# A hybrid decoder step on one core: order of the first loads, pacing of VectorE's convolution, a later norm, and two copies moved to ScalarE

## The chip, the cores and the metric

The kernel runs on one core of a Trainium2 chip. The metric is the device time of one execution in microseconds (us). PE is TensorE (PEld its weight loads), DVE is VectorE, ACT is ScalarE, POOL is GpSimd, and SP is the queue that issues most of the DMAs.

## The reference, cut to what matters

One layer of a decoder trunk over 16 meta tokens and 512 prompt tokens, and 8 sequences of 4 sample tokens (560 tokens in all), width 1024:

```python
proj = rmsnorm(h) @ w_in                 # [q | k | v | z | a | b | glu_in]
qkv = silu(causal_dwconv(qkv, 4 taps))   # then l2norm of q and k per head
# gated delta rule, 4 heads of 128, prompt in chunks:
L = strict(kb @ k.T * decay);  sol = solve(I + L, [v * beta | kb * exp(G)])
v_new = u_v - w_k @ S;  o = (q * exp(G)) @ S + (q @ k.T * decay) @ v_new
S = S * exp(G_last) + (k * exp(G_last - G)).T @ v_new
# the other 512 channels:
c = causal_dwconv(glu, 31 taps) + b;  c = silu(layernorm(c))
h = h + [o, c] @ w_out
h = h + peer(rmsnorm(h))                 # top-k over 128 x 128 experts, dense over all of them
```

## The kernel before, in words

The work is done in stages. (1) **Head**: five tiles of 112 rows of x are loaded, squared and normalised, transposed on PE, and split into a high and a low part in fp32r (ACT writes the high part with `xhigh`, DVE the low part with `xlow`). Weights come in blocks of up to 256 columns; `high(b)` on ACT and `low(b)` on DVE split block b in the same way, and PE makes three products a tile. (2) **Blocks 0 to 7**: the scalars a and b, the first glu block, and six q/k/v blocks, back to back on PE; ACT evacuates each unit (half of the tokens for 128 columns), DVE makes the 4-tap convolutions. After a block, `scalars(b)` makes one part of the gates or of the row norms of q and k. (3) **Mixer**: blocks 8 to 12 (glu 1, glu 3, glu 2, z, z) and the delta rule of five chunks (chunk 0 of 48 rows, chunks 1 to 4 of 128), the sample sequences, the layer norm of the convolution, and the first output units. (4) The output and query projections, the top-k, and (5) a dense pass over the experts with their gathers, about two thirds of the time.

In the mixer every engine runs one fixed order. Each strand of work (a chunk, the sample tokens, the norm, the late blocks) is a generator that yields the name of its next step, and `side_by_side` takes the step with the smallest **turn**, a hand-written number. A chunk's step has the turn `FIRST[ci] + LEVEL[n]`, with FIRST 4.2, 13.5, 30.5, 41.3 and 44.8. Half a unit of a late block takes one turn (`lin` + 0.6), so the five late blocks fill turns 0.6 to 39.6. The norm's steps stand in `NORM_AT`: `ls` (PE sums over channels, 46), `lc` (DVE subtracts the mean), `lv0` to `lv3` (ACT squares a channel tile at the same turn at which PE wants it), `lr`, `lm`, `ln` (49.6). All engines share the turns, and a semaphore per engine counts finished steps.

The 31-tap convolution of four channel tiles is 4 x 31 = 124 **pieces** on DVE, one instruction over 528 columns each (L1892 and L1894). `CONV_BY` gives how many are done after each of the blocks 2 to 7; block 7 brings them to 31. In the mixer, `feed` adds up to two pieces after every DVE step while the turn is under 40 and one after that, as far as the glu blocks so far allow (31 pieces for each). The sample tokens' taps (`conformer_seqs`) follow inside `glu`: one product over 992 columns, a reduction, a bias.

The inverse of a chunk's triangular block is built from powers: `p2`, `p4`, `p8` and their transposes `pt2`, `pt4`, then `n`, `nt`, `n2`, `nt2`, `nt4`. PE makes each in a PSUM bank, and ACT copies the plain ones into SBUF, DVE the transposed ones, `nt4` apart. `free_bank` makes PE wait until the engine named in `chunk_groups` has read a bank's earlier content.

At the end of block 7, the last `scalars` on PE makes the column sums for the row norms of q and k (one-column products, L949); DVE adds eps, ACT takes the square root, DVE inverts (`row_scales`, L1856), all in the first turns of the mixer.

## Time and profile before

| what | value |
|---|---|
| runs | 1883.71 us median of 3 (1883.66 to 1886.05) |
| the profiled execution | 1889.95 us, span of its trace 1888.2 us |
| PE / PEld busy | 95% / 93% of the span |
| DVE busy | 74% |
| ACT / POOL busy | 38% / 36% |
| mean granted TensorE clock | 0.975 |

Busy shares are averages over stages with different limits, so the stages have to be read one at a time: the granted clock and the busy time of each engine in a stretch, and which wait ends last at a step. A granted clock of 1.00 is 2.4 GHz and 0.50 is 1.2 GHz; a value between is a mixture of both within the stretch.

### The profile page before, as it was taken

The page shows a single profiled execution, that of the slowest core. Times are in us where ns is not written, and L with a number is a line of the kernel's source. Part 1 is how long each engine was busy: PE and PEld are TensorE (multiplying, and loading weights), DVE is VectorE, ACT ScalarE, POOL GpSimd, SP SyncE. Part 2 cuts the span into 40 slices and gives each one's busy share as a digit, 9 for nine tenths or more (in the row PEclk, how much of TensorE's full clock was granted, in tenths as well). Part 3 has the DMA queues.
Part 4 walks back from the last instruction along what each step waited for, and adds up shares of the span by engine and source line. Part 5 has one row for each costly group of instructions (what it writes and reads, how often), then busy time and mean ns, then how long its engine had stood idle before and what let it go on. Part 6 is the DMA issues. An engine that isn't in the chain of part 4 may idle for free.

```text
span 1888.2 us, 29407 instructions
## 1 busy us (share of the span) xinstructions
PE 1802.2 (95%) x11505; PEld 1752.5 (93%) x11505; DVE 1393.0 (74%) x2528; ACT 712.0 (38%) x1244; POOL 672.4 (36%) x438
## 2 busy tenths in 40 slices
PE   6997879799899999999999999999999999999998
PEld 5997779789899999999999999999999999999997
DVE  4876896565499999999966657526878788887753
ACT  4535333642333343334344333333333333333332
POOL 3000000000000467868777677771344333333100
PEclk9988899889999999999999999999999999999999
DMA  7211001045132368888998989999999999999831
GB/s 209 68 45 45 32 1 52 1 100 151 41 112 90 126 238 277 266 294 298 321 312 302 314 291 308 316 329 403 322 387 379 348 341 359 357 340 345 318 115 37
DMA packets 190706, 424.33 MB, mean 225 GB/s; under 512 B 11162, under 2 KB 119222, under 8 KB 180320
## 3 DMA queue, kind: packets, MB, share of 16 engines
q1 hardware_dynamic: 153256, 287.47, 44.0%
q0 software_dynamic: 37312, 134.97, 20.4%
q8 instruction: 92, 1.51, 0.3%
q14 instruction: 46, 0.38, 0.1%
HBM read 360.76 MB, written 62.06 MB: 224 GB/s over the span
## 4 chain that ended last, share of the span: by engine, by line
PE 59%; DVE 15%; issue 2%; POOL 1%; ACT 0%; DMA 0%; DVEq 0%; POOLq 0%
PE psum L1292 31%; PE psum L1271 21%; PE psum L1259 3%; PE psum L901 3%; DVE junk L2395 2%; DVE besti L2258 1%; DVE sring L2262 1%; DVE besti L2270 1%; DVE best L2266 1%; DVE best L2254 1%; PE psum L906 1%; DVE oh L2385 1%; DVE WR L1786 1%; DVE eqx L2322 1%; DVE pick L2333 1%
## 5 line engine op out<-in xcount | busy, mean ns | idle before, releaser
L1271 PE MATMUL psum<-xT,WS 128*128 128x416 f32 x3072 | 595.0, 353 | 4.6 <-POOL WS L841 4.6
L1292 PE MATMUL psum<-AR,WS 128*128 128x416 f32 x3072 | 580.5, 350 | 2.6 <-DVE AR L2466 2.6
L1292 PEld LDWEIGHTS psum<-AR,WS 128*128 128x128 f32 x3072 | 574.2, 187 | 8.9 <-DVE AR L2466 3.0
L1271 PEld LDWEIGHTS psum<-xT,WS 128*128 128x128 f32 x3072 | 572.1, 188 | 10.6 <-POOL WS L841 6.2
L841 POOL TENSOR_TENSOR WS<-RAWP,WS 128x1024 fp32r<-128x1024 f32 x128 | 309.7, 2430 | 720.8 <-ACT WS L1686 620.2
L906 PE MATMUL psum<-xT,WR 128*128 128x280 f32 (+1 forms) x1968 | 282.2, 304 | 15.0 <-DVE ss L1795 7.8
L832 POOL DMA_INDIRECT rowg<-in_expert_v,idx x128 | 182.5, 1426 | 315.4 <-DVE acc L2409 307.6
L906 PEld LDWEIGHTS psum<-xT,WR 128*128 128x128 f32 x1968 | 270.4, 200 | 16.7 <-DVE ss L1795 8.1
L1696 ACT ACTIVATE WS<-RAWP 128x1024 fp32r<-128x1024 f32 x128 | 135.6, 1059 | 332.5 <-PE psum L1292 332.5
L2459 DVE TENSOR_TENSOR WS<-RAWP,WS 128x1024 fp32r<-128x1024 f32 x128 | 156.7, 1224 | 114.6 <-ACT WS L1696 114.6
L1723 ACT ACTIVATE actA<-psum 128x416 f32<-128x416 f32 x128 | 66.4, 519 | 404.9 <-PE psum L1271 404.6
L2395 DVE CUSTOM_DVE_ANT_0 junk<-rowg,psum 128x1024 bf16<-128x1024 f32 x128 | 155.9, 1218 | 51.2 <-DMA rowg<-in_expert_u_rows,idx 43.3
L832 POOL DMA_INDIRECT rowg<-in_expert_u_rows,idx x128 | 165.9, 1296 | 41.0 <-issue 22.8
L2409 DVE SCALAR_TENSOR_TENSOR acc<-rowg,coef,acc 128x1024 f32<-128x1024 f32 x128 | 163.9, 1281 | 2.9 <-DMA rowg<-in_expert_v,idx 0.5
L2385 DVE TENSOR_TENSOR oh<-iotab,pairs 128x2048 bf16<-128x2048 bf16 x52 | 96.1, 1847 | 91.8 <-PE psum L1259 90.9
L1686 ACT ACTIVATE WS<-RAWP 128x1024 fp32r<-128x1024 f32 x128 | 134.4, 1052 | 0.0
L1894 DVE SCALAR_TENSOR_TENSOR cT<-gext,dwcols,cT 128x528 f32<-128x528 f32 x120 | 92.3, 769 | 4.2
L2388 DVE TENSOR_TENSOR ohg<-oh,pairs 128x3072 bf16<-128x3072 bf16 x52 | 91.5, 1759 | 1.8
L2457 DVE TENSOR_TENSOR act<-act,Gt 128x416 f32<-128x416 f32 x128 | 74.9, 585 | 13.0 <-DMA act<-act_dram 9.5
L1748 ACT ACTIVATE AR<-act 128x416 fp32r<-128x416 f32 x128 | 69.0, 539 | 39.0 <-DVE act L2457 39.0
L2466 DVE TENSOR_TENSOR AR<-act,AR 128x416 fp32r<-128x416 f32 x128 | 74.9, 585 | 6.6 <-ACT AR L1748 6.5
L1259 PE MATMUL psum<-ohg,oh 128*128 128x128 bf16 x1248 | 78.7, 219 | 0.0
(373 smaller groups left out, 1610.2 us busy)
## 6 DMA issues: line engine op xcount, KB each, us to landing
RAWP<-in_expert_u SPq DMA_DIRECT2D x64, 1024.0 KB, 6.8
RAWP<-in_expert_v SPq DMA_DIRECT2D x64, 1024.0 KB, 7.9
act_dram<-actA SPq DMA_DIRECT2D x128, 208.0 KB, 4.3
gate_dram<-gblk SPq DMA_DIRECT2D x26, 1024.0 KB, 10.4
act<-act_dram SPq DMA_DIRECT2D x64, 416.0 KB, 8.3
Gt<-gate_dram SPq DMA_DIRECT2D x16, 1664.0 KB, 9.7
RAW<-in_w_in SPq DMA_DIRECT2D x8, 1024.0 KB, 5.4
RAW<-in_w_query SPq DMA_DIRECT2D x8, 1024.0 KB, 8.4
```

Of the source, the lines that this page charges most:

```text
L832: pool.indirect_dma_start(out=rowg[:, s_ % 4, :], out_offset=None, in_=table, in_offset=bass.IndirectOffsetOnAxis(ap=idx[:, s_ % PAIRS:s_ ...
L841: pool.tensor_tensor(ws(n)[:, 1], raw(n), ws(n)[:, 0].bitcast(F32), ALU.subtract).then_inc(u_low, 1)
L906: last = mm(bank[u % 4][:, 0:hw], W[:, pw, kt, m * P:(m + 1) * P], xT[:, px, kt, side * hw:(side + 1) * hw], **go)
L1259: last = mm(bank[4 + g % GBANKS][:, k * NK:(k + 1) * NK], oh[:, b % 2, 0, i, :], ohg[:, b % 2, x, i, :], start=(x == 0), stop=(x == 2))
L1271: last = mm(bank[e % 2][:, 0:TD], ws(e)[:, pw, kt * P:(kt + 1) * P], xT[:, px, kt, TSP:TPE], start=(kt == 0 and i == 0), stop=(kt == KT - ...
L1292: last = mm(bank[dt][:, 0:TD], ws(NK + e)[:, pw, dt * P:(dt + 1) * P], AR[:, e % 4, pa, :], start=(e == 0 and i == 0), stop=(e == NK - 1 a ...
L1686: act.activation(ws(n)[:, 0], raw(n), ACT.Copy).then_inc(u_high, 1)
L1696: act.activation(ws(n)[:, 0], raw(n), ACT.Copy).then_inc(v_high, 1)
L2385: chain(tt(by_two(oh[:, i]), keys_, per_token(0, 2), ALU.is_equal))
L2395: dve.tensor_tensor_reduce(junk[:], rowg[:, s_ % 4, :], xnP, 1.0, 0.0, ALU.mult, ALU.add, sdot[:, s_:s_ + 1]).then_inc(dot_done, 1)
L2409: dve.scalar_tensor_tensor(acc[:], rowg[:, s_ % 4, :], coef[:, s_:s_ + 1], acc[:], ALU.mult, ALU.add).then_inc(axpy_done, 1)
L2459: tt(ws(NK + e)[:, 1], raw(NK + e), ws(NK + e)[:, 0].bitcast(F32), ALU.subtract).then_inc(v_low, 1)
```

## The change: what it does

- SP issues all five row tiles of x before the weights of block 0 (before: the weights stood between tiles 2 and 3). POOL issues its two large small-parameter loads (`sconf`, `sqkv`) last, and waits for the last row tile before them. ACT and DVE take the rows of tiles 3 and 4 ahead of the split of block 0.
- The row norms of q and k: PE's last sums come after the second unit of block 7, `row_squares` on DVE between the block's two channels, ACT's roots and the last two SiLUs before `high(9)`, and `row_scales` after `low(9)` and ahead of the mixer.
- DVE's late work in pieces: `low` of blocks 10, 11 and 12 in four parts at turns 1.5 apart; the sample taps of a late glu in two products, a turn apart, and a reduction at a third turn.
- Taps by places: block 7 no longer brings the pieces to 31 (they stay at 26), and `feed` follows `due(turn)`, with at most 3 pieces a step.
- The norm of the convolution starts at turn 48.5 and not at 46, and its squares get turns of their own, ahead of the sums; `onb` and `on` of the first three outputs move back with it.
- The copies of `pt2` and `nt2` go from DVE to ACT.

```diff
-CONV_BY = {2: 5, 3: 10, 4: 16, 5: 21, 6: 26, 7: CC}
+CONV_BY = {2: 5, 3: 10, 4: 16, 5: 21, 6: 26}
...
-                  "onb": {SAMPLE: 47.2, 1: 48.2, 2: 49.2, 3: 56.1, 4: 59.2},
-                  "on": {SAMPLE: 47.9, 1: 48.9, 2: 49.9, 3: 56.6, 4: 60.5}}
-        NORM_AT = {"ls": 46, "lc": 46.05, "lv0": 47.1, "lv1": 47.6, "lv2": 48.1, "lv3": 48.6, "lr": 48.7,
-                   "lm": 49.1, "ln": 49.6}
+                  "onb": {SAMPLE: 48.9, 1: 50.1, 2: 51.1, 3: 56.1, 4: 59.2},
+                  "on": {SAMPLE: 49.6, 1: 50.7, 2: 51.7, 3: 56.6, 4: 60.5}}
+        NORM_AT = {"ls": 48.5, "lc": 48.55, "sq0": 49.3, "sq1": 49.35, "lv0": 50.3, "lv1": 50.8, "sq2": 50.85,
+                   "lv2": 51.3, "sq3": 51.32, "lv3": 51.75, "lr": 51.85, "lm": 52.3, "ln": 52.8}
...
-                 ("pt2", (V, "pt2")), ("t1", (V, "t1")), ("p4", (A, "p4")), ("pt4", (V, "pt4")), ("t2", (V, "t2")),
+                 ("pt2", (A, "pt2")), ("t1", (V, "t1")), ("p4", (A, "p4")), ("pt4", (V, "pt4")), ("t2", (V, "t2")),
...
-                g += [("n", (A, "n")), ("nt", (V, "nt")), ("n2", (A, "n2")), ("nt2", (V, "nt2")),
+                g += [("n", (A, "n")), ("nt", (V, "nt")), ("n2", (A, "n2")), ("nt2", (A, "nt2")),
...
             for t in range(NTB):
                 load_rows(t)
-                if t == 2:
-                    load_weights(0)
+            load_weights(0)
...
+                    (dtb[:, 0:HEADS], dt_bias.to_broadcast([P, HEADS])),
+                    (dtb[:, HEADS:], a_log.to_broadcast([P, HEADS])),
                     (sconf[:], state_conf[0].rearrange("(r b) t c -> (b t) r c", r=2)),
-                    (sqkv[:], state_qkv[0].rearrange("b t c -> (b t) c")),
-                    (dtb[:, 0:HEADS], dt_bias.to_broadcast([P, HEADS])),
-                    (dtb[:, HEADS:], a_log.to_broadcast([P, HEADS]))):
+                    (sqkv[:], state_qkv[0].rearrange("b t c -> (b t) c"))):
+                if n == 8:
+                    pool.wait_ge(x_in[NTB - 1], 16)
                 pool.dma_start(dst, src).then_inc(small_in, 16)
...
-                linear(b)
-                scalars(b)
+                if b == LATE - 1:
+                    linear(b, lambda n: scalars(LATE - 1) if n == 1 else None)
+                else:
+                    linear(b)
+                    scalars(b)
...
             xhigh(1, 1)
-            high(0)
-            xhigh(1, 2)
             square(1, 4)
             root(1, 4)
+            xhigh(1, 2)
+            high(0)
...
-                while done < 2 * sum(x[0] == "qkv" for x in BLOCKS[:b]):
+                if b == LATE - 1:
+                    V.wait(act, "qk2")
+                    fn(tok[:, RQ], tok[:, RQ], ACT.Sqrt)
+                    fn(tok[:, RK], tok[:, RK], ACT.Sqrt, "rqk")
+                while done < 2 * sum(x[0] == "qkv" for x in BLOCKS[:b + (b == LATE - 1)]):
...
+                yield "pt2", ci
+                if ci:
+                    V.wait(act, "Lo", ci)
+                take("pt2", M[3][0:c, :, 0:c])
...
+                yield "nt2", ci
+                take("nt2", M[5][:])
...
+            xnorm(1, 3)
+            xlow(1, 2)
             low(0)
-            xlow(1, 2)
-            xnorm(1, 3)
...
+            def late_lows():
+
+                for b in range(LATE + 1, first["out"] - 1):
+                    n = sum(x[2] for x in BLOCKS[b + 1][2])
+                    for i in range(4):
+                        yield ("lin", 2 * (UNIT0[b] - UNIT0[LATE]) + 1.6 + 1.5 * i), LIN
+                        A.wait(dve, "high", b + 1)
+                        k = slice(2 * i, 2 * i + 2)
+                        op(tt(WR[:, (b + 1) % 2, 1, k, 0:n], RAW[:, SLOT[b + 1], k, 0:n],
+                              WR[:, (b + 1) % 2, 0, k, 0:n].bitcast(F32), ALU.subtract), "low", b + 1)
+
+            def late_glus():
...
+                        yield ("lin", k + 8.5), LIN
+                        glu(b)
+                        yield ("lin", k + 9.9), LIN
+                        for i in range(2):
+                            if i:
+                                yield ("lin", k + 10.9), LIN
+                            seqs_product(c, 4 * i, 4 * i + 4)
+                        yield ("lin", k + 11.9), LIN
+                        seqs_sum(c)
...
-                yield "pt2", ci
-                op(dve.tensor_copy(sq_(M[3]), src("pt2")), "pt2", ci)
...
-                    if n == "r1":
-                        yield "nt2", ci
-                        op(dve.tensor_copy(sq_(M[5]), src("nt2")), "nt2", ci)
...
+            def due(at_):
+
+                return 26 + int(min(max(at_ - 5, 0), 5) + 2 * min(max(at_ - 9.6, 0), 18.4)
+                                + 2.6 * min(max(at_ - 28, 0), 12) + 3.2 * max(at_ - 40, 0))
+
             def feed(at_):

-                conv_to(min(pieces[0] + (2 if at_ < LINEAR_END else 1), CC * gated[0]))
+                conv_to(min(max(pieces[0], due(at_)), pieces[0] + 3, CC * gated[0]))
```

## Rows read from the trace of the kernel before

**Rows 1.** Windows: stretch, length, busy PE PEld DVE ACT POOL, PEclk, DMA, GB/s.

```profile
38.00:143.00 105.00, 105.00 (x780) 103.95 (x779) 81.52 (x129) 46.78 (x119) 0.00 (x0) 0.93 0.25 70
521.00:630.00 109.00, 109.00 (x868) 108.94 (x867) 105.57 (x590) 39.63 (x75) 10.40 (x5) 1.00 0.25 85
```

**Rows 2.** Windows of the mixer, same columns, cut at the glu and chunk boundaries.

```profile
143.30:168.10 24.80, 20.23 (x157) 18.77 (x157) 11.93 (x29) 17.71 (x40) 0.00 (x0) 0.86 0.15 43
168.10:188.00 19.90, 14.83 (x105) 12.45 (x103) 16.77 (x25) 3.91 (x11) 0.00 (x0) 0.74 0.16 54
188.00:209.00 21.00, 18.26 (x137) 17.59 (x137) 17.14 (x26) 13.05 (x36) 0.00 (x0) 0.92 0.00 1
209.00:252.70 43.70, 33.08 (x221) 30.95 (x220) 39.88 (x56) 8.01 (x15) 0.00 (x0) 0.92 0.10 35
252.70:270.60 17.90, 11.21 (x75) 11.02 (x74) 17.34 (x25) 4.15 (x8) 0.00 (x0) 0.81 0.00 0
270.60:306.20 35.60, 35.12 (x275) 34.05 (x275) 29.03 (x41) 13.88 (x35) 0.00 (x0) 1.00 0.01 2
306.20:337.60 31.40, 31.22 (x232) 29.99 (x231) 15.91 (x26) 15.45 (x43) 0.00 (x0) 0.89 0.29 77
337.60:365.40 27.80, 20.22 (x114) 17.34 (x113) 10.79 (x27) 15.94 (x54) 0.00 (x0) 0.85 0.00 0
365.40:396.00 30.60, 28.21 (x169) 25.79 (x169) 21.15 (x32) 16.98 (x42) 0.00 (x0) 0.80 0.07 18
396.00:435.60 39.60, 31.30 (x196) 28.55 (x195) 26.75 (x42) 18.09 (x47) 0.00 (x0) 0.87 0.46 110
```

**Rows 3.** Timeline of the head: start, length, engine, instruction [idle before, releaser].

```profile
9.94 1.06 ACT L1314 ACTIVATE sq<-h 112x1024 f32<-112x1024 f32 x1 [0.58 <-DMA h<-in_x_prompt]
...
18.28 1.06 ACT L1314 ACTIVATE sq<-h 112x1024 f32<-112x1024 f32 x1 [6.00 <-DMA h<-in_x_prompt]
...
24.04 3.14 PE L906 MATMUL psum<-xT,WR 128*128 128x280 f32 x12 [7.81 <-DVE ss L1795]
...
36.49 0.81 PEld L865 LDWEIGHTS psum<-ident,sqkv 24*128 24x128 f32 x12
```

**Rows 4.** Windows of the head, columns as in rows 1.

```profile
10.00:18.30 8.30, 4.39 (x21) 3.35 (x19) 3.38 (x5) 2.27 (x6) 5.26 (x27) 1.00 1.07 209
```

**Rows 5.** DMA issues of the first 20 us: KB each, us to landing.

```profile
sconf<-in_state_conf_conv POOLq DMA_DIRECT2D x1, 480.0 KB, 11.1
```

**Rows 6.** Timeline of the mixer, columns as in rows 3.

```profile
152.78 0.88 PE L1007 MATMUL psum<-tri_m,tok 48*48 48x48 f32 x8 [4.57 <-DVE tok L1861]
...
159.77 0.45 PE L1014 MATMUL psum<-ident,KH 48*128 48x48 f32 x4
...
215.78 2.05 PE L1000 MATMUL psum<-M,M 128*128 128x128 f32 x8 [5.22 <-DVE M L2035]
...
263.54 2.05 PE L1084 MATMUL psum<-VN,KE 128*128 128x128 f32 x8 [6.69 <-DVE VN L2075]
```

**Rows 7.** Groups by line and form, 143 to 436 us: count, busy, mean ns, idle before.

```profile
L1894 DVE SCALAR_TENSOR_TENSOR cT<-gext,dwcols,cT 128x528 f32<-128x528 f32 x95 | 73.0, 769 | 3.4
...
L1314 ACT ACTIVATE M<-psum 128x512 f32<-128x512 f32 x32 | 18.9, 595 | 69.5 <-PE psum L1000 61.2 <-PE psum L1076 4.7 <-PE psum L1023 3.6
...
L1786 DVE TENSOR_TENSOR WR<-RAW,WR 128x2048 fp32r<-128x2048 f32 x5 | 11.4, 2287 | 1.3 <-ACT WR L1314 1.3
...
L1157 PE MATMUL psum<-csq,ones 128*128 128x280 f32 x16 | 6.7, 555 | 7.6 <-ACT csq L1314 7.6
...
L2183 DVE RECIPROCAL psum<-psum 128x280 f32<-128x280 f32 x2 | 3.8, 1910 | 0.0
```

**Rows 8.** Groups by form of DVE alone, 306 to 436 us, same columns.

```profile
L2172 DVE SCALAR_TENSOR_TENSOR cT<-psum,cT 128x280 f32<-128x280 f32 x8 | 2.9, 437 | 3.5 <-PE psum L1157 3.5
...
L2192 DVE TENSOR_TENSOR xT<-cT,xT 128x512 fp32r<-128x512 f32 x4 | 2.5, 685 | 0.0
...
L2035 DVE COPY M<-psum 128x512 f32<-128x512 f32 x2 | 1.4, 692 | 0.7 <-PE psum L1000 0.6
```

45 lines of the change are left out of this document (19 added, 26 removed).

## The prediction

> **What bounds the kernel now.** I went from the windows (which engine is full in which stage) to the table of waits, and from there to the timeline at each place that the change touches. In blocks 0 to 7 PE is busy for all of 105.0 us with DVE at 81.5 [rows 1]: PE sets the pace there, so whatever starts that stage earlier moves it as a whole. In the top-k stage PE shows 109.0 of 109.0 and DVE 105.6 [rows 1]; both are full, nothing of the change lies there, and it has to follow the mixer. The expert passes come after it and are untouched. So a microsecond won at the end of the mixer (436 us) is a microsecond of the run, and the question is what the head and the mixer lose.
>
> The head loses its time to one load. ACT squares row tile 2 at 9.94 us, and then stands for 6.00 us until tile 3 has landed at 18.28 [rows 3]. Tile 3 was queued behind the weights of block 0, and POOL's two large loads share the same engines. ACT's order is fixed, so `xhigh` of tile 1 and the split of block 0 stand behind that square, and PE's first real product starts at 24.04 after a wait of 7.81.
>
> In the mixer no engine is full over the whole, but they are full by turns [rows 2]. The reader is to see three kinds of stretch. From 168 to 253 us DVE is busy for 16.8 + 17.1 + 39.9 = 73.8 of 84.6 us while PE is so for 66.2, at a granted clock of 0.74 and 0.92: DVE's backlog makes PE wait, for 5.22 us at 215.8 (`pt2`'s copy, behind a glu, its taps and pieces) and once more for 6.69 at 263.5 (`ws`, same cause) [rows 6]. After such a wait PE runs at 1.2 GHz for a while, which a stretch shows as a clock below 1.00. From 270.6 to 306.2 PE is busy for 35.1 of 35.6 at clock 1.00 with DVE at 29.0: the best that the two do together. From 306 to 436 DVE has room (74.6 of 129.4 by the last four rows) and PE has stops of its own, among them 7.6 us before the products on `csq`, released by ACT [rows 7].
>
> **The change, part by part.**
>
> *Rows of x first: -4 us.* Tile 3 is 448 KB. Behind tile 2 at 9.94, and at no more than the 209 GB/s of that stretch [rows 4], it lands after 2.2 us, at about 12.1; tile 4 after as much again, 14.3; block 0's 512 KB at about 16.8. ACT then is never short of a tile: it ends `xhigh` of tile 0 at 12.3, squares tile 3 to 13.7, `xhigh` 1 to 14.7, squares tile 4 to 16.2, `xhigh` 2 to 17.3 and the split of block 0 to 18.4. DVE follows with `low(0)` to 19.8, and PE starts at 19.9 where it was 24.04. The bound from below is 3 us (weights 1 us later), from above 5. What could take it back is POOL's `sconf` and `sqkv`: issued at about 14.5 and with the landing of before, 11.1 us [rows 5], they are there by 27.5, and PE asks for them at 36.49 less 4.1 = 32.4 [rows 3]. Five microseconds of cover; without it the head would lose what they are late. POOL's masks move by some 6 us behind the same wait, and are wanted first at 69 us.
>
> *End of block 7: -2 us.* Before, PE stands for 4.57 us ahead of 152.78, because five pieces (5 x 0.77 us) [rows 7] lie ahead of the row norms on DVE [rows 6]. Now `gb` waits for nothing. But the new order makes ACT do two roots, four SiLUs and `high(9)` in a row after the last unit, and DVE's `low(9)` and `row_scales` wait for that. By the durations in this case (unit to 144.0, roots 1.7, SiLUs to 149.5 since the last needs the last convolution, split 1.9, low 2.3, scales 1.2) the masks of chunk 0 start at about 154.9, against some 154.4 before (152.78, the scales 1.2, semaphores): DVE's side starts no earlier. PE gains since `gb` and `k` are long done by then and nothing runs at half clock: `khT` at 156.4 against 159.77 [rows 6]. The one-column products now fall inside block 7, and the clock falls after such products even though PE never stops (0.93 over 38 to 143) [rows 1]; up to 1.7 us of the 3.4, half of one unit's time, may go there. Between 0 and 3.4 I take 2.
>
> *Pieces by places, taps and lows in parts, pt2 and nt2 on ACT: -18 us.* I count DVE's work of each stretch again. Between 143 and 306 there ran 98 pieces (95 of 0.769 us [rows 7] and three first ones of another form); `due` leaves 73 of them, by the turns at the six stretches' ends 4, 6, 10, 16, 9 and 28. Four DVE copies of 0.69 (one of them of chunk 0, 0.35) [rows 8] leave as well. The split lows cost more: four instructions of 512 columns took 2.5 us [rows 8] against 2.29 for one of 2048 [rows 7], so +0.2 a block. So DVE goes from 132 to about 111 us over the 162.9. PE's own 132.7 busy us hold up to (1 - clock) of each stretch as half-clock time, 17 us; at full clock it needs 116. By stretch, (DVE, PE) needs: 168 to 188 (11.3, 9.7), to 209 (15.6, 16.6), to 252.7 (25.8, 29.6), to 270.6 (15, 8), to 306.2 (30.6, 35.1). Neither fills a stretch completely, since a chunk's step goes back and forth between engines. With 80 to 87% for the fuller one, as now, I take 13, 19, 35, 17 and 35.6 for 19.9, 21.0, 43.7, 17.9 and 35.6: gains of 7, 2, 8.5, 1 and 0, or 18.5. From below: only the stops named in rows 6 go (5.2 + 6.7 and half of it again in clock), and the rest is replaced by other waits, -8. From above: DVE as full throughout as at 270 to 306 (29.0 of 35.6, 0.82), 111 / 0.82 = 136 for 162.9, so -27.
>
> The Trainium skill speaks against splitting: "VectorE: DVE Perf Modes", section on the TRN2 errata, holds that every instruction pays a fixed cost and gives (N + 151) / 0.96 ns for an fp32 tensor_tensor, to be met with larger tiles. By it a low in four parts takes 2.76 us, 0.47 more each and 1.4 us over three blocks; the row has 0.2 each, 0.6 us. Either is small beside 18, so the sum keeps the row's.
>
> *The copies on ACT* add 9 x 0.6 us there (an ACT copy of 512 columns took 595 ns) [rows 7], where it is busy for 60.7 of 162.9 and 66.5 of 129.4 us [rows 2]. What can cost is not the load but the queue: `pt2` may stand behind `high` (1.9 us) or an exponent group (2.4). PE has a half unit of 1.6 to 1.8 us in between. I take 0; if every one were late by 1 us it would be +9.
>
> *Deferred pieces and the later norm, 306 to 436: +1 us.* The 25 pieces (19.2 us) now stand at turns 40 to 48. In 306.2 to 337.6, DVE goes from 15.9 to about 29.8 of 31.4 us [rows 2], where PE is already full: I take +4. In 337.6 to 365.4 the stop before `csq` (7.6 us) goes, since the squares have turns ahead of the sums: -7. The norm's own work goes later and lands among chunk 4's steps: 3.8 us of reciprocals and 2.9 of the subtraction, with eight more products like those for the scale, some 9.6 us on DVE [rows 7, 8], and on PE the sums over `cT` and the 6.7 over `csq` [rows 7]. They stood in someone's way before too (at chunk 3's steps); I put +4 for it. Bounds: -8 (DVE's holes take it all) and +15.
>
> **The sum.** -4 - 2 - 18 + 1 = -23 us. The profiled execution of before was 1889.95 (span 1888.2), so this one would be 1867; it lies 6.2 above the median, and against the median of 1883.7 the same sum gives 1861.
>
> **The rivals.**
>
> *Tail gives it back (smaller gain).* DVE's holes after 306 are where chunk 3 and 4 get their quick answers; a piece or two (0.8 to 1.5 us) ahead of each answer delays a chain with no half units left to hide it. Then the tail costs +8 to +12, and the whole is -8 to -14: about 1872. For it: PE is at 31.2 of 31.4 there. Against: PE full means that an answer is often early.
>
> *Slower.* The same mechanism to the end: all 25 pieces and the norm's 9.6 us on the path of chunks 3 and 4, 28.8 us, with the stop before `csq` only moved, against 24 won elsewhere: +5, about 1889. It decides once more than 24 of the 28.8 us lie on the path. Against it: DVE was idle for 54.8 us after 306 [rows 2].
>
> *The mixer starts behaving as at 270 to 306 everywhere.* Fewer stops, no half clock: -4 - 2 - 27 - 7 = -40 (the last for `csq`, all else in the tail hidden), about 1844. For it: every clock below 1.00 follows a stop. Against it: chunk 0's small products leave little to overlap.
>
> *The order does nothing in the mixer*, because turns are only an order, and PE waits for ACT's copies in place of DVE's: the head's 4 us alone, and 0 to 2 more: 1878. Or even less, if `sconf` is late as well: no change.
>
> **How the numbers follow.** The range and the chances come from the cases. A difference of 0.2%, 3.8 us, is about what this kernel's measurement can tell from none. Forecast (-16 to -31): 0.58. Tail gives back (-8 to -15): 0.18. Head alone (-4 to -8): 0.06. More than -31: 0.07. Within 3.8: 0.05. Slower: 0.06. So faster 0.89, same 0.05, slower 0.06. The likeliest case has 1853 to 1868. From 1848 to 1876 is -36 to -8, which holds all but 2 in 10.
>
> **What the profile after would show.** Head: ACT's square of tile 3 with no wait over 1 us, PE's first product with fp32r weights at 20 us, the constants at 32. Block 7's end: no stop of PE before `gb`; chunk 0's first masks no earlier than before, once 4 us are taken off. Mixer: 73 pieces by the last late unit and 25 after it, DVE near 111 us to there, PE's clock above 0.95, and its last late unit at about 281 (before: 306). Tail: no wait for `csq`; the stretch from there to the end of chunk 4's `su` 130 us long, give or take 4. The prediction is wrong if that last stretch grows by over 8, if PE's clock from 168 to 253 stays near 0.9, or if `pt2` and `nt2` on ACT show up as what PE waits for.

## The result and the profile after

The changed kernel took 1868.98 us (median of 4 runs, 1866.35 to 1871.53), the one before 1883.91; the ratio is 0.9921 with an interval of 0.9892 to 0.9949. That is 15 us less, where 23 were forecast and 1861 predicted; the range of 1848 to 1876 holds it. The profiled execution took 1871.53 us with a span of 1869.8, against a span of 1888.2 before, so the two spans differ by 18.4 us. It goes by stage like this:

| stage (spans of one execution each) | before | after | difference | forecast |
|---|---|---|---|---|
| start to block 1 on PE | 38.15 | 31.76 | -6.4 | -4 |
| blocks 1 to 7 | 105.15 | 103.84 | -1.3 | 0 |
| first to last late unit | 162.9 | 142.1 | -20.8 | -20 |
| last late unit to first output unit | 129.4 | 138.3 | +8.9 | +1 |
| all after it | 1452.6 | 1453.9 | +1.3 | 0 |

**The head.** This is ACT's timeline, then PE's, of the kernel after; they answer to [rows 3].

```profile
11.72 1.06 ACT L1318 ACTIVATE sq<-h 112x1024 f32<-112x1024 f32 x1
...
14.15 1.06 ACT L1318 ACTIVATE sq<-h 112x1024 f32<-112x1024 f32 x1
...
16.39 1.06 ACT L1318 ACTIVATE WR<-RAW 128x1024 fp32r<-128x1024 f32 x1
```

```profile
18.75 3.08 PE L907 MATMUL psum<-xT,WR 128*128 128x280 f32 x12 [3.18 <-DVE WR L1793]
...
30.11 0.92 PE L866 MATMUL psum<-ident,sqkv 24*128 24x24 f32 x12
30.95 1.04 PE L870 MATMUL psum<-ident,sconf 120*128 120x120 f32 x8
31.76 6.42 PE L907 MATMUL psum<-xT,WR 128*128 128x280 f32 x48
```

The squares of tiles 3 and 4 stand at 11.72 and 14.15 with no bracket behind them: ACT waits for no tile. `sqkv` and `sconf` are there when PE asks at 30.11, so POOL's later issue is hidden. PE stands at block 1 at 31.76, 6.4 us earlier.

**The mixer.** The windows of the kernel after, cut at the same events as [rows 2], to within some 1.5 us (columns as there):

```profile
135.60:158.50 22.90, 19.29 (x149) 17.90 (x148) 10.37 (x22) 17.46 (x42) 0.00 (x0) 0.85 0.16 47
158.50:170.30 11.80, 11.66 (x113) 9.84 (x110) 9.12 (x17) 4.72 (x12) 0.00 (x0) 1.00 0.01 1
170.30:192.30 22.00, 18.06 (x127) 17.37 (x127) 17.81 (x28) 12.92 (x36) 0.00 (x0) 0.84 0.14 48
192.30:227.40 35.10, 32.83 (x238) 30.72 (x237) 28.95 (x48) 10.15 (x18) 0.00 (x0) 1.00 0.13 43
227.40:235.70 8.30, 8.30 (x70) 8.24 (x70) 8.09 (x12) 3.54 (x8) 0.00 (x0) 1.00 0.01 2
235.70:277.70 42.00, 37.21 (x275) 36.38 (x274) 36.12 (x51) 14.37 (x37) 0.00 (x0) 0.92 0.01 1
277.70:308.00 30.30, 28.72 (x208) 27.37 (x206) 23.23 (x36) 14.52 (x40) 0.00 (x0) 0.89 0.29 79
308.00:333.80 25.80, 16.88 (x105) 15.29 (x105) 20.57 (x36) 12.78 (x48) 0.00 (x0) 0.77 0.00 1
333.80:372.00 38.20, 37.87 (x238) 33.12 (x239) 20.69 (x32) 18.67 (x52) 0.00 (x0) 0.93 0.10 29
372.00:416.00 44.00, 31.15 (x157) 27.86 (x155) 27.61 (x47) 23.05 (x53) 0.00 (x0) 0.71 0.37 87
```

In the second window PE is full at clock 1.00 for 11.8 us, where it had 14.83 busy of 19.9 at 0.74. From 192.3 to 235.7 the clock is 1.00 throughout and PE busy for 41.1 of 43.4 us; the same two windows took 61.6 us before. The last window ahead of the tail went the other way: 42.0 us where it was 35.6. The last four windows are the tail: PE at 16.88 of 25.8 with DVE at 20.57, and a clock of 0.71 in the last one, against 0.87 before.

What PE waited for (engine and line, releaser: us in total, times, longest), first from 136 to 280, then from 279 to 416 us, of the kernel after:

```profile
PE psum L1018 <- DVE KH L2045: 11.6, 3, 4.5
PE psum L1004 <- ACT M L1318: 1.2, 2, 0.8
```

```profile
PE psum L1052 <- DVE RA L2096: 4.0, 1, 4.0
...
PE psum L1128 <- ACT KE L1318: 2.8, 1, 2.8
...
PE psum L1161 <- DVE cT L1906: 1.7, 1, 1.7
```

The stops of 4.57, 5.22 and 6.69 us of [rows 6] have gone. In the late stretch nothing above 1.2 us is left but KH, which has grown: 11.6 us where PE waited 2.5 us for it before. The 7.6 us of [rows 7] ahead of the sums over `csq` are no longer in the tail's list. In their place stand 4.0 us for RA, 1.7 ahead of the sums over `cT`, and smaller ones in the steps of the sample rows. The stop for RA stands behind the norm's own reciprocals and products on DVE (DVE, then PE):

```profile
370.17 3.87 DVE L2207 RECIPROCAL psum<-psum 128x280 f32<-128x280 f32 x2
374.07 2.94 DVE L2210 TENSOR_TENSOR cT<-cT,psum 128x280 f32<-128x280 f32 x8
376.93 0.68 DVE L2096 TENSOR_TENSOR RA<-RB,psum 128x512 f32<-128x512 f32 x1
```

```profile
377.66 2.08 PE L1052 MATMUL psum<-RA,M 128*128 128x256 f32 x4 [3.96 <-DVE RA L2096]
```

### The profile page after: what moved, and what is told of

Same layout as the page of the kernel before. It is cut to its first block, busy times and chain, and to the rows that moved or that the text cites. A ratio compares the mean times of both kernels' runs of the same rounds, so it can differ in the third digit from the quotient of the medians.

```text
span 1869.8 us, 29423 instructions
## 1 busy us (share of the span) xinstructions
PE 1798.9 (96%) x11505; PEld 1748.5 (94%) x11505; DVE 1383.7 (74%) x2531; ACT 715.1 (38%) x1252; POOL 673.4 (36%) x438
## 4 chain that ended last, share of the span: by engine, by line
PE 58%; DVE 16%; issue 2%; DMA 2%; POOL 1%; ACT 1%; DVEq 0%; POOLq 0%; ACTq 0%
PE psum L1296 29%; PE psum L1275 21%; PE psum L1263 3%; PE psum L902 3%; DVE junk L2424 2%; DMA act<-act_dram 2%; DVE besti L2287 1%; DVE sring L2291 1%; DVE besti L2299 1%; DVE best L2295 1%; DVE best L2283 1%; PE psum L907 1%; DVE WR L1793 1%; DVE oh L2414 1%; DVE eqx L2357 1%
## 5 line engine op out<-in xcount | busy, mean ns | idle before, releaser
L907 PE MATMUL psum<-xT,WR 128*128 128x280 f32 (+1 forms) x1968 | 276.0, 300 | 10.4 <-DVE xT L1820 7.2
L907 PEld LDWEIGHTS psum<-xT,WR 128*128 128x128 f32 x1968 | 264.4, 196 | 12.0 <-DVE xT L1820 7.8
L833 POOL DMA_INDIRECT rowg<-in_expert_u_rows,idx x128 | 166.1, 1298 | 37.4 <-issue 22.5
L2486 DVE TENSOR_TENSOR act<-act,Gt 128x416 f32<-128x416 f32 x128 | 74.9, 585 | 15.9 <-DMA act<-act_dram 12.3
```

What stands on the lines that cost most here:

```text
L833: pool.indirect_dma_start(out=rowg[:, s_ % 4, :], out_offset=None, in_=table, in_offset=bass.IndirectOffsetOnAxis(ap=idx[:, s_ % PAIRS:s_ ...
L907: last = mm(bank[u % 4][:, 0:hw], W[:, pw, kt, m * P:(m + 1) * P], xT[:, px, kt, side * hw:(side + 1) * hw], **go)
```

## The experiments

These marks stay the same in every kernel: E7 (a moment, not the run e7) is ACT's last `qtail` copy, which ends block 7's convolution input, and gb1, gb3 are PE's first products of chunks 1 and 3. Where a run starts its late blocks depends on the execution by some 5 us (with the new head, E7 stood between 135.96 and 141.38), so stages are read from E7 on. "Out" is the first output unit. The stages are read to about 0.1 us, from one profiled execution of each kernel.

| kernel | ratio to before, interval | E7 to gb1 | gb1 to gb3 | gb3 to out | E7 to out |
|---|---|---|---|---|---|
| before | 1 | 46.4 | 119.9 | 127.8 | 294.1 |
| e1 head alone | 0.9968, 0.9951 to 0.9986 | 46.1 | 120.3 | 127.0 | 293.4 |
| e5 places alone | 1.0015, 0.9997 to 1.0034 | 39.7 | 115.4 | 140.7 | 295.8 |
| e2 old rule in after | 1.0066, 1.0041 to 1.0091 | 43.6 | 133.4 | 127.3 | 304.3 |
| e12 whole and DVE | 0.9966, 0.9945 to 0.9987 | 37.4 | 114.1 | 132.1 | 283.6 |
| e9 whole | 0.9944, 0.9925 to 0.9963 | 35.3 | 110.7 | 135.4 | 281.4 |
| e10 lows whole | 0.9922, 0.9894 to 0.9950 | 32.9 | 108.2 | 136.7 | 277.8 |
| e3 copies on DVE | 0.9923, 0.9897 to 0.9950 | 33.0 | 110.6 | 131.2 | 274.8 |
| e7 copies by chunk | 0.9938, 0.9922 to 0.9953 | 34.3 | 108.9 | 136.8 | 280.0 |
| e4 norm back | 0.9929, 0.9904 to 0.9954 | 32.9 | 108.7 | 136.7 | 278.3 |
| e6 done by turn 40 | 0.9944, 0.9927 to 0.9960 | 33.0 | 110.9 | 132.7 | 276.6 |
| after | 0.9921, 0.9892 to 0.9949 | 34.3 | 108.9 | 136.7 | 279.9 |
| e8 scales first | 0.9888, 0.9857 to 0.9919 | 31.7 | 105.6 | 133.2 | 270.5 |
| e11 low(9) late | 0.9923, 0.9898 to 0.9949 | 29.0 | 107.7 | 133.4 | 270.1 |

**e1, the head alone.** The four hunks of the head (SP's queue, POOL's order and wait, ACT's and DVE's order) put into the kernel before:

```diff
                 load_rows(t)
-                if t == 2:
-                    load_weights(0)
+            load_weights(0)
...
+                if n == 8:
+                    pool.wait_ge(x_in[NTB - 1], 16)
```

> The kernel before with the head's part alone: the load queue's order, the two halves of ACT's and DVE's order that go with it, and the later sconf and sqkv. Theory: the head's 6.4 us are carried through as a shift, since PE is full in blocks 1 to 7 (105 us busy of 105) and the mixer is a chain that starts when block 7 ends. The linear of block 1 starts at 31.8 us on PE in place of 38.2, the first late unit and everything after it 6 to 7 us earlier, ratio 0.9966, some 1877.5 us. Rival: the gain is only to be had with the new end of block 7, and the mixer's queues absorb it; then the last late unit stays within 2 us of 306.2 and the ratio is 0.999 or more.

Measured: ratio 0.9968, about 6 us; block 1 on PE at 32.56, the first output unit at 429.4 in place of 435.6. The head's gain passes through the whole mixer as a shift, and nothing from E7 on changes (293.4 against 294.1). The theory holds.

**e2, the old rule for the pieces in the kernel after.**

```diff
-CONV_BY = {2: 5, 3: 10, 4: 16, 5: 21, 6: 26}
+CONV_BY = {2: 5, 3: 10, 4: 16, 5: 21, 6: 26, 7: CC}
...
-                conv_to(min(max(pieces[0], due(at_)), pieces[0] + 3, CC * gated[0]))
+                conv_to(min(pieces[0] + (2 if at_ < LINEAR_END else 1), CC * gated[0]))
```

> The kernel after with one thing undone: the pieces of the conformer's taps are fed two a turn while the late units run and one a turn behind them, and the rest of the first 31 at the end of block 7 (behind the row scales), as before the change. Theory (the pieces by places make the gain of the late stretch): the stretch from the first late unit to the last one (142.1 us after the change, 162.9 before) grows by 12 to 16 us, DVE's busy time there from 110 to some 128, and the tail behind it (138.3 after, 129.4 before) comes down by 5 to 9; together +7 us against the kernel after, about 1876, ratio 0.996. Rival A (the taps and lows in parts and the copies on ACT make the gain): the late stretch stays within 4 us of 142 and the tail still comes down, 1862 to 1866, ratio 0.990. Rival B (the tail's loss is the later norm's): the late stretch grows by 12 or more and the tail stays at 138, about 1883, ratio 1.000.

It was slower than the kernel before, which no theory had: 1.0066. The tail came down as the first theory said, to 127.3, but the late stretch grew by far more than 16 us. The pieces alone on DVE in chunk 0's products and in chunk 1's first steps (windows: length, DVE busy with pieces and their count, PE's clock, DMA share, GB/s) of this kernel, then of the one before in the same steps:

```profile
156.10:183.70 27.60, 10.99 (x15) 0.81 0.00 1
183.70:206.70 23.00, 12.08 (x16) 0.58 0.14 46
```

```profile
159.80:187.90 28.10, 8.46 (x11) 0.82 0.12 38
187.90:203.10 15.20, 6.19 (x9) 0.89 0.01 1
```

31 pieces where there were 20: the old rule gives two at every turn, and splitting lows and taps made more turns. The pieces bunch, the clock falls to 0.58, and later, ahead of chunk 2's `khT`, PE's longest single wait (for KH) is 14.6 us (waits of PE from 160 to 318):

```profile
PE psum L1018 <- DVE KH L2045: 20.0, 2, 14.6
```

So this run does not measure what the rule by places is worth in the kernel before; it shows that the split lows and taps cannot go with the old rule.

**e3, `pt2` and `nt2` back on DVE.**

```diff
-                 ("pt2", (A, "pt2")), ("t1", (V, "t1")), ("p4", (A, "p4")), ("pt4", (V, "pt4")), ("t2", (V, "t2")),
+                 ("pt2", (V, "pt2")), ("t1", (V, "t1")), ("p4", (A, "p4")), ("pt4", (V, "pt4")), ("t2", (V, "t2")),
...
+                yield "pt2", ci
+                op(dve.tensor_copy(sq_(M[3]), src("pt2")), "pt2", ci)
```

> The kernel after with the copies pt2 and nt2 back on DVE. Theory: the copies are worth little either way: nine copies of 0.35 to 0.69 us come back to DVE, five in the late stretch where DVE is near full, so +2 us there, and in the tail 0 to -1: 1871, ratio 0.993. Rival: ACT's queue is what PE waits for since the copies stand in it (ACT's waits in the tail are 12 us each on M); then this kernel is faster than the one after, by 3 to 6 us in the tail: 1865, ratio 0.990.

0.9923 in all: no difference from the kernel after. E7 to gb3 is 143.6 against 143.2. By the time of the run the copies are worth nothing as long as the rest of the change is there; the part on the late stretch, below, shows what they do to PE's stops. The tail of this execution is 5.5 us shorter, which e7 tests.

**e4, the norm at its old places.**

```diff
-        NORM_AT = {"ls": 48.5, "lc": 48.55, "sq0": 49.3, "sq1": 49.35, "lv0": 50.3, "lv1": 50.8, "sq2": 50.85,
-                   "lv2": 51.3, "sq3": 51.32, "lv3": 51.75, "lr": 51.85, "lm": 52.3, "ln": 52.8}
+        NORM_AT = {"ls": 46, "lc": 46.05, "lv0": 47.1, "lv1": 47.6, "lv2": 48.1, "lv3": 48.6, "lr": 48.7,
+                   "lm": 49.1, "ln": 49.6}
...
-                    yield f"sq{c}", NORM
+                    yield f"lv{c}", NORM
```

> The kernel after with the conformer's norm at its old places (from turn 46 on, the squares at the turns of their sums), so that the six pieces that are not yet done by turn 46 are done in one go there. Theory (the deferred pieces are what costs in the tail): the norm's place is worth little: the stop ahead of the sums over csq (7.6 us before) is back, chunk 4's steps gain some 7 us, and the tail from the last late unit to the first output unit stays within 3 us of 138.3; 1869, ratio 0.992. Rival (the later norm costs): the tail comes down by 6 to 9 us to about 131, 1861, ratio 0.988.

0.9929, the same within the interval, and the tail as long as in the kernel after. But PE's waits from 282 to 419 are others:

```profile
PE psum L1161 <- DVE cT L1906: 9.3, 1, 9.3
PE psum L1161 <- ACT csq L1318: 7.6, 3, 4.4
```

17 us of stops ahead of the norm's products in place of 1.7. The kernel after has in their place the 4.0 us for RA, which this one lacks, small stops, and more of PE's half clock (below). The first theory had the total right.

**e5, the pieces by places alone**, in the kernel before (the function `due`, the new `feed`, no entry for block 7):

```diff
-                conv_to(min(pieces[0] + (2 if at_ < LINEAR_END else 1), CC * gated[0]))
+                conv_to(min(max(pieces[0], due(at_)), pieces[0] + 3, CC * gated[0]))
```

> The kernel before with the pieces by places alone (the rule due, no pieces at the end of block 7); lows and taps whole, norm and copies as before, head as before. In the run with the old rule in the changed kernel the pieces bunched (31 between chunk 1's gb and the products after it, against 19 before, since the old rule counts turns and the change has more of them), so that run overstates the rule's worth; this one is the clean measure. Theory (the rule makes most of the late stretch's gain, and the pieces it defers make the tail's loss): from chunk 0's khT to the last late unit 144.5 us before, some 132 here (127.7 with everything); from there to the first output unit 131.3 before, 138 to 141 here; in all -4 to -8 us against before, ratio 0.997. Rival A (the rule needs the split lows and taps to act): the first stretch stays over 140, ratio 1.000 or above. Rival B (the tail's loss is not of the pieces): tail at 131 to 133, ratio 0.992.

No gain at all: 1.0015. E7 to gb3 shrinks by 11.2 us, to 155.1, and the tail grows by 12.9. The wait ahead of the norm tells why (waits of PE from 294 to 436):

```profile
PE psum L1157 <- DVE cT L1894: 9.9, 1, 9.9
```

The deferred pieces end 9.9 us too late for a norm that is still at turn 46. Neither of the stated cases holds whole: the time is rival A's, but from `khT` to the last late unit it took 139.2 us, just under that rival's 140, and the tail behind it 144.1, longer than in any case. Deferring the pieces and moving the norm belong together, as far as one trace of each tells: with the norm moved as well (e12, which also has the new head and the new end of block 7, both ahead of this stretch) the tail is 132.1 in place of 140.7.

**e6, all pieces due by turn 40.**

```diff
-                                + 2.6 * min(max(at_ - 28, 0), 12) + 3.2 * max(at_ - 40, 0))
+                                + 4.7 * min(max(at_ - 28, 0), 12) + 3.2 * max(at_ - 40, 0))
```

> The kernel after with a steeper rule from turn 28 on (4.7 pieces a turn in place of 2.6), so that all 124 pieces are due by turn 40 and none is left for the tail. Theory (a deferred piece costs 9/25 us in the tail): the tail comes down from 140.1 to some 131 us; the stretch from chunk 0's khT to the last late unit grows from 127.7 by less than the 19 us that the pieces last, since DVE was busy for 29 of 35.6 us there: +5 to +9; net 0 to -4 us against the kernel after, ratio 0.991. Rival (the tail's loss is due to something else, the copies on ACT or the split of the norm): tail stays near 140 and this kernel is 5 to 9 us slower than the one after, ratio 0.996.

0.9944, from 0 to 4 us slower than the kernel after, while its profiled execution was 4 us faster: inconclusive on the total. In the trace 41 pieces stand between gb2 and gb3 (30 after), 17 between the gb of chunks 3 and 4 (9), none behind. Their price moved with them: +2.0 us from gb1 to gb3, and the stretch from chunk 3's gb to chunk 4's took 27.8 us in place of 18.1, the next, up to the norm's first sums, 30.5 in place of 36.4. Neither case had it: from the last late unit to the first output unit it is 136.2 us where 131 was expected and the kernel after has 140.2, and the ratio lies nearer to the rival's.

**e7, copies by ACT for chunks 0 to 2 and by DVE for 3 and 4.**

```diff
-                prod4("p4", M[3], M[2], (A, "pt2"))
+                prod4("p4", M[3], M[2], (A if ci < 3 else V, "pt2"))
...
+                if ci >= 3:
+                    yield "pt2", ci
+                    op(dve.tensor_copy(sq_(M[3]), src("pt2")), "pt2", ci)
```

> The kernel after with pt2 and nt2 copied by ACT for chunks 0 to 2 and by DVE for chunks 3 and 4. In the run with all of them on DVE the tail was 134.6 us against 140.1, and the late stretch (khT to last late unit) 128.1 against 127.7. Theory (in the tail ACT's queue is what a copy stands in): tail 134 to 136, late stretch 127 to 128, so -5 us against the kernel after, ratio 0.989. Rival (that difference was the scatter of single executions): tail at 138 to 141, ratio 0.992.

0.9938 and a tail of 136.8: the rival is right. In the tail this kernel has e3's copies and not its time, so the copies did not make the short tail of e3, and the difference has a place. One stretch, from chunk 3's `wT` to chunk 4's, lasts 23.5 or 23.6 us in the kernel after, e7, e9 and e10, and 19.7 to 20.2 in e2, e3, e6, e8, e11 and e12. Here it is in the kernel after and in e8 (windows, all columns):

```profile
379.50:403.10 23.60, 19.84 (x106) 17.91 (x105) 10.47 (x18) 9.35 (x29) 0.00 (x0) 0.77 0.67 156
```

```profile
374.50:394.40 19.90, 16.13 (x105) 14.80 (x104) 10.48 (x18) 9.34 (x29) 0.00 (x0) 0.92 0.72 168
```

The same work and the same busy DVE; only PE's clock differs, 0.77 and 0.92. These 3.7 us go with no part of the change. That there is half clock at all does come with the change: in both kernels it begins at PE's stop of 3.96 us for RA, and by windows of 2 us it lasts some 13 us in the kernel after and 6 in e8. All ten of the kernels named have that stop just ahead (3.95 or 3.96 us, 2.30 in e6), and all have the later norm. Those with the norm at its old places (before, e1, e4, e5) do not have it, and take 18.4 to 18.9 us for the stretch.

**e9, lows and taps whole again** (e10: the lows alone).

```diff
-                    for i in range(4):
-                        yield ("lin", 2 * (UNIT0[b] - UNIT0[LATE]) + 1.6 + 1.5 * i), LIN
-                        A.wait(dve, "high", b + 1)
...
+                    yield ("lin", 2 * (UNIT0[b] - UNIT0[LATE]) + 1.2), LIN
+                    low(b + 1)
...
-                        yield ("lin", k + 9.9), LIN
-                        for i in range(2):
...
-                            seqs_product(c, 4 * i, 4 * i + 4)
+                        seqs_product(c, 0, NSEQ)
```

> The kernel after with the lows and the taps of the sample rows whole again in the late blocks; the pieces still come by places. The pieces by places alone won little (1.0015), and there PE still stopped between khT and chunk 1's gb: 1.94 us ahead of products on M, behind a whole taps (1.97 and 1.19 us) and a glu on DVE, and 0.67 us behind a whole low of 2.27 us. Theory (the pieces by places only pay where nothing longer than a piece stands ahead of a chunk's answers, so the split makes the late gain together with them): khT to gb of chunk 1 goes from 21 to 26 or 27 us, gb of chunk 1 to gb of chunk 3 from 109 to 114 or more, in all +9 to +12 against the kernel after: 1879 to 1882, ratio 0.998. Rival (the copies on ACT or the end of block 7 made it): ratio within 0.002 of 0.992 to 0.994, and khT to gb of chunk 1 stays at 21 to 22.

> The kernel after with only the lows whole again (one subtraction of 2.27 us a block in place of four of 0.69), taps in halves. Theory: a low comes three times in the late blocks and stands ahead of one or two answers each time; it accounts for 3 to 5 us of what the split wins, the taps for the rest: ratio 0.995. Rival: only the taps matter, since they stand ahead of chunk 0's t1 and the low comes behind it; ratio as the kernel after, 0.992 to 0.994.

Whole lows alone cost nothing in the run (0.9922): e10's rival holds and its theory does not. With whole taps too the ratio is 0.9944, 0.9925 to 0.9963, an interval that overlaps e10's and that of the kernel after; in the trace E7 to gb3 is 146.0, 2.8 us more than after and 4.9 more than in e10. e9's theory (0.998, +9 to +12 us) lies outside the interval, and its rival's ratio holds; from `khT` to gb1 it is 23.2 us, between the rival's 21 to 22 and the theory's 26 to 27.

**e12, both undone:** the lows and taps of e9 with the copies of e3.

> The kernel after with both undone: lows and taps whole, and pt2 and nt2 copied by DVE. Each alone cost little (ratio 0.9944 and 0.9923, the kernel after 0.9921), yet the pieces by places without either, without the new end of block 7 and without the later norm gained nothing (1.0015 without the new head, which alone gives 0.9968). Theory (either one is enough to keep DVE's queue short ahead of a chunk's answers, so one covers for the other): khT to gb of chunk 1 goes to 26 us or more (20.9 and 23.2 with one of them undone, 27.3 with pieces alone), gb of chunk 1 to gb of chunk 3 to 114 or more (110.7, 115.4), ratio 0.997 to 0.999, some 1880. Rival (the end of block 7 and the norm's place make the rest of the gain, and the copies are worth nothing in any company): khT to gb of chunk 1 at 23, the next stretch at 111, ratio 0.994 to 0.995, some 1875.

0.9966, E7 to gb3 151.5: 8.3 us more than in the kernel after, where each one alone cost 2.8 and 0.4. The theory comes closest, at or just short of its lower end (0.997, and 26 us from `khT` to gb1, where 25.3 were measured). PE's timeline and DVE's show what a stop is made of (the sum is chunk 0's):

```profile
169.10 0.89 PE L1004 MATMUL psum<-M,M 48*48 48x48 f32 x16 [1.96 <-DVE M L2051]
```

```profile
163.40 0.70 DVE L1970 TENSOR_TENSOR gext<-gext,gate 128x528 f32<-128x528 f32 x1
...
164.42 1.97 DVE L1881 TENSOR_TENSOR taps<-gext,dwcols 128x992 f32<-128x992 f32 x1
166.43 1.19 DVE L1887 TENSOR_REDUCE cT<-taps 128x32 f32<-128x992 f32 x1
...
168.61 0.34 DVE L2051 TENSOR_TENSOR M<-M,psum 48x192 f32<-48x192 f32 x1
```

A sum of 0.34 us for which PE stands stood behind 5.2 us of work (163.40 to 168.61) for which nobody was waiting. And the two largest waits of [rows 6] are back (waits of PE from 140 to 290):

```profile
PE psum L1004 <- DVE M L2049: 7.1, 2, 5.2
...
PE psum L1088 <- DVE VN L2089: 4.0, 1, 4.0
```

L2049 is `pt2`'s copy. With the copies on ACT and lows and taps whole (e9) PE waited 6.2 us for `t1`'s sum in its place (longest 4.9), and 4.1 for VN. With the taps in parts neither stop is there, with the copies on DVE (e3) or on ACT (the kernel after, e10). So the two large stops go with the whole taps, whoever makes the copies.

**e8, the row scales ahead of low(9).** In the kernel after, DVE stands for 3.64 us ahead of `low(9)`, for ACT's `high(9)`, with the scales and chunk 0's masks behind it, and PE then stands as long ahead of `khT`, 7.9 us behind its gb at 140.17:

```profile
143.35 2.29 DVE L1793 TENSOR_TENSOR WR<-RAW,WR 128x2048 fp32r<-128x2048 f32 x1 [3.64 <-ACT WR L1318]
...
146.82 0.35 DVE L2042 TENSOR_TENSOR M<-psum,pos_m 48x192 f32<-48x192 f32 x1
```

```profile
148.08 0.66 PE L1018 MATMUL psum<-ident,KH 48*128 48x48 f32 x4 [3.61 <-DVE KH L2045]
```

```diff
+                if b == LATE - 1:
+                    row_scales()
                 low(b + 2)
                 scalars(b)
-                if b == LATE - 1:
-                    row_scales()
```

> The kernel after with the row scales ahead of low(9) and the scalars at the end of block 7. DVE stands there for 3.64 us for ACT's high(9), with the row scales, the masks and chunk 0's KH behind it, and PE then waits 3.61 us for KH. Theory: KH is there some 3.5 us earlier, PE's stop before khT goes, and chunk 0's khT stands 4 to 5 us behind gb in place of 7.9; what follows moves by 3 us, ratio 0.990 to 0.991. Rival: low(9) and the masks only change places, and the gain of 3 us is lost by the first late units or chunk 0's own exps; khT to chunk 1's gb grows by what was won, ratio 0.992.

0.9888, 0.9857 to 0.9919: the best of all and below the interval of e7 on the same chip (0.9922 to 0.9953), though not clear of the kernel after's own (0.9892 to 0.9949). The stated step gave less than expected: gb to `khT` 6.7 us in place of 7.9, since `low(9)` still stood ahead of the masks. E7 to gb1 is 31.7 (32.9 to 34.3 in the kernels that share the code of both stretches with the one after), gb1 to gb3 105.6 (108.7 to 108.9), and the tail was one with the higher clock. Only the first is the mechanism of the edit; whether the second follows from it was not settled.

**e11, low(9) behind chunk 0's masks as well.**

```diff
-                for b in range(LATE + 1, first["out"] - 1):
+                for b in range(LATE, first["out"] - 1):
...
+                        at_ = 1.6 + 1.5 * i if b > LATE else 3.7 + 0.8 * i
```

> The kernel after with the row scales first at the end of block 7 and low(9) in four parts behind chunk 0's masks and KH. With the scales first but low(9) still ahead of the masks the ratio was 0.9888, and PE still stopped for 2.35 us ahead of chunk 0's khT, for DVE had 2.29 us of low(9) ahead of the masks and waited 2.38 us for ACT's high(9) before it. Theory: masks of chunk 0 start 4 us earlier, when k's transposes are done, KH is there when PE asks, khT stands 4 to 5 us behind gb in place of 6.7, and 2 us go: ratio 0.988, some 1861. Rival: ACT's exps of chunk 0 stand behind high(9) anyway, and PE stops ahead of kk instead for as long; ratio 0.989 to 0.990.

In the mixer it did what the theory said: `khT` 4.2 us behind gb, with PE waiting for nothing there and 1.08 us ahead of the next step, on ACT's copy of KHT:

```profile
147.64 0.45 PE L1018 MATMUL psum<-ident,KH 48*128 48x48 f32 x4
148.01 1.80 PE L907 MATMUL psum<-xT,WR 128*128 128x280 f32 x12
150.90 0.56 PE L1021 MATMUL psum<-KHT 128*48 128x48 f32 x8 [1.08 <-ACT KHT L1318]
```

Neither theory had the run right. E7 to gb1 is 29.0, 5.3 less than after, and E7 to out 270.1, the shortest. Yet the ratio is 0.9923: everything behind the first output unit took 1460.4 us in its profiled execution, against 1453.0 in e8 (1451.4 to 1457.2 in all other kernels). The two expert passes hold 7.3 of the 7.4 us: 664.2 and 608.6 us against 662.2 and 603.3, with the same instructions (before: 664.2 and 601.7). In the second pass PE stops once more some 105 us from its start, for DVE, which had stood for 12.45 us for a load of activations (DVE, then PE):

```profile
1362.74 0.59 DVE L2488 TENSOR_TENSOR act<-act,Gt 128x416 f32<-128x416 f32 x1 [12.45 <-DMA act<-act_dram]
```

```profile
1366.23 5.98 PE L1296 MATMUL psum<-AR,WS 128*128 128x416 f32 x22 [2.32 <-DVE AR L2497]
```

In e8 DVE's wait is 9.9 us and the second stop of PE is not there. All the kernels sort by it: with 9.0 to 10.1 us, in ten of them, PE has no second stop and the pass takes 600.5 to 603.3 us; with 12.3 or 12.4 (the kernel after, e4, e11) PE stops for 2.0 to 2.3 us and it takes 605.3 to 608.6; e10 lies between (10.7, a stop of 1.0, 603.1). The rest of e11's 5.3 us is a lower clock, 0.97 in the 50 us around the stop and 0.94 in the first 50 us of the pass, 1.00 and 0.97 in e8. In the first pass PE waits 4.3 us for POOL's WS in place of 2.7. Why the load lands later in some executions stays open: e11 has the shorter mixer and is no faster kernel.

## Why the prediction was right in sign and short in size

**Head, -4: right in mechanism, under-sized, -6.4** (e1: -6.0 in the run). I took the 209 GB/s of [rows 4] for the tiles' arrival; the new order moved 275 GB/s from 10 to 18.3 us, so tile 3 was there when ACT asked and PE's first product stood at 18.75, not 19.9. The other 1.1 us lie between PE's first product and its second wait, which is 1.44 us in both kernels: 8.7 us before, 7.6 after; what shortened them stays open. The 5 us of cover for `sconf` held.

**End of block 7, -2: right.** e5 and e12 share the pieces by places, whole lows and taps and the copies on DVE; e12 adds the new end of block 7 (and the head, ahead of E7, and the later norm, behind gb3). E7 to gb1 is 39.7 and 37.4: -2.3, where kernels with the same code there differ by up to 1.4 (32.9 to 34.3). The step "DVE's side starts no earlier" held as well: the masks stand at 146.82, 7.6 us earlier than before, and the head and blocks 1 to 7 alone give 7.7. The stop did not go; it moved from gb (4.57) to `khT` (3.61), and e11 took it away.

**Late stretch, -18: right in total (-20.8 with the end of block 7, forecast -20), the composition not foreseen, and in part luck.** DVE's busy time was 110.46 us (forecast 111), and 70 pieces were done in it and 29 behind it (forecast 73 and 25). By windows the forecast was 13, 19, 35 + 17 and 35.6 us, and 11.8, 22.0, 35.1 + 8.3 and 42.0 were measured: the forecast is 1.2 and 8.6 us too long in two places and 3.0 and 6.4 too short in two, and these cancel. The last window has DVE at 36.1 of 42.0 us and the longest stop for KH, 4.5 us, which no term of the prediction held.

From the kernel before to the one after, E7 to gb3 goes 166.3, 155.1 with the places (e5), 151.5 with the end of block 7 (e12), 146.0 with the copies on ACT (e9), 143.2 with lows and taps in parts (after). Take the copies away last and the stretch grows by 0.4 us, the parts 2.8, both together 8.3. That looks as if the savings did not add. PE's busy time in the same stretch says otherwise (windows from E7 to gb3, all columns: after, e3, e9, e12):

```profile
136.00:279.30 143.30, 128.55 (x967) 121.56 (x966) 111.97 (x177) 63.22 (x148) 0.00 (x0) 0.93 0.08 26
```

```profile
139.80:283.50 143.70, 126.27 (x967) 118.96 (x966) 113.80 (x181) 62.45 (x145) 0.00 (x0) 0.95 0.08 26
```

```profile
140.50:286.50 146.00, 125.84 (x966) 118.61 (x965) 111.11 (x164) 63.16 (x148) 0.00 (x0) 0.95 0.08 26
```

```profile
139.40:290.90 151.50, 129.03 (x967) 121.45 (x966) 113.48 (x168) 62.20 (x145) 0.00 (x0) 0.93 0.08 25
```

The stretch less PE's busy time is the time in which PE stands: 14.7, 17.4, 20.2 and 22.5 us. In the kernel after, e4 and e7, which share the code here, it is 14.7 each time. So the copies take away 2.7 us of standing, the parts 5.4 and both 7.7: the stops add. What does not is PE's busy time, which is 128.5, 126.9 and 128.5 us in the three kernels with the same code, by the clock. The excess that looked like an overlap is of this kind. The parts also have a price within the 5.4: the half taps, the reduction and the quarter lows now fall ahead of KH, and PE waits 11.6 us for KH where e9 has 5.5. Of the two, the taps are the longer item: with the lows whole and the taps in parts (e10) PE stands for 16.1 us, 1.4 more than in the kernel after.

"VectorE: DVE Perf Modes" of the Trainium skill, section on the TRN2 errata, has the formula by which a split low is estimated at 4 x 0.69 = 2.76 us against 2.29; the trace has 12 parts of 687 ns, 2.75 us for four, so the page's price is right here and my +0.2 a block from [rows 8] was too low. The page's advice, tiles of 512 elements or more, is just met by the parts of 512 columns, so it did not speak against this split; and e10, with each low in one piece again, saved nothing in the run.

**Copies on ACT, 0: right.** PE waited 1.2 us in total for ACT's M in the late stretch; neither e3 nor e7 is clear of the kernel after in the run.

**The tail, +1: wrong, +8.9.** This is the step that failed: "Deferred pieces and the later norm: +1", the sum of +4, -7 and +4. By the prediction's own mark ("wrong if that last stretch grows by over 8") it is the rival *tail gives it back* that holds for this stretch, while the rest of the sum was larger than forecast. The 15 us of the medians are that rival's as well (-8 to -15); the 18.4 us of the spans are the likeliest case's (-16 to -31). That the sum held is therefore luck in part. The -7 came true as a wait that is gone, and was replaced: the norm kept 6.8 us of reciprocals and products on DVE, and at its new place they stand ahead of RA, for which PE stops for 3.96 us and then runs at half clock. The +4 put for the norm's work was mis-sized. What the runs put in place of the +1: without deferred pieces and with the norm late the stretch from gb3 to out is 127.3 (e2, against 127.8 before); with deferred pieces and the norm late it is 131.2 to 133.4 in the runs with the higher clock (e3, e6, e8, e11, e12), so deferring costs some 5 us; with the norm left at 46 it is 140.7 (e5). In e6 only 17 pieces stand behind gb3, where the kernel after has 28, and its 132.7 are no less, so the price does not simply follow their number. Apart from these 5 us, the sums over `cT` have grown: PE stops ahead of them for the last piece, 1.66 us, and they take 6.63 us against 3.94 before, at a clock of 0.60 against 1.00. They are slow in e2 as well (5.9 us), within its 127.3. On top of the 5 us come, in the kernel after, the 3.7 us of longer half clock between the `wT` of chunks 3 and 4 (in three other kernels too). The later norm itself brings nothing without deferral (e2), and up to 8.6 us with it (e12 against e5). Taken back out of the kernel after (e4) it is worth less, at most 3.7 once the clock of the stretch is allowed for, and nothing in the run.

**PE's clock above 0.95: half right.** From 158.5 to 235.7 it was 0.95 by the windows above (0.84 for 22.0 us, 1.00 for the rest), over the whole late stretch 0.93. Ahead of most of the rest stand the three waits for KH, 11.6 us, which I had not named: each chunk's masks and KH stand behind pieces on DVE as everything else does, and PE asks for them at a fixed turn.

**The sum.** -6.4 - 1.3 - 20.8 + 8.9 + 1.3 = -18.3 in the spans, -14.9 in the medians; the difference is that the profiled execution of before lay 6.0 us above the median of 1883.91 and that of after 2.6 above its own.

## What to carry to other kernels

When filler work is put between an engine's awaited answers, look for the longest item that can stand ahead of an answer: whole taps brought back two stops of 4 to 5 us. Split it, and see what the parts now stand ahead of (KH, 5.5 to 11.6 us). Undo savings both alone and together, and count the waiting engine's idle time apart from its busy time: the lengths of a stage (0.4 and 2.8 us alone, 8.3 together) suggested an overlap, while the idle time added up (2.7 and 5.4 alone, 7.7 together) and repeated to 0.1 us in kernels with the same code. A rule that deals out filler work per turn changes its rate when anything else is split into more turns; tie it to places, as a first step, or the split costs more than it wins (1.0066). Work that is deferred has a deadline at its consumer: move the consumer in the same change, or the deferral is paid back there (9.9 us ahead of the norm in e5). A consumer that is moved brings its own work along: look at whose answer it now stands ahead of (6.8 us ahead of RA).
